# The first norm's shift and scale: from column sums on VectorE to TensorE products in column groups, block by block

## The chip, the cores and the metric

One core of a Trainium2 chip runs the whole program. The metric is the time of one execution on the device in microseconds (us), as the median of the runs. TensorE is the matmul engine, VectorE (DVE), ScalarE (ACT) and GpSimd (POOL) are the elementwise engines, SyncE (SP) issues most transfers.

## The reference

Two transformer blocks over 256 tokens of width 1024. Only the opening of the first one matters here:

```python
mx = (silu(c) @ ada_w + ada_b).reshape(b, 1, 6, D)      # c: (1, 1024), ada_w: (1024, 6144)
mc = (silu(c_ctx) @ ada_w + ada_b).reshape(6, D)
hx = modulate(rmsnorm(x, norm1_g), mx[:, :, 0], mx[:, :, 1])    # h * (1 + scale) + shift
hc = modulate(rmsnorm(ctx, norm1_g), mc[0], mc[1])
ux = hx @ w_in          # w_in: (1024, 4608)
uc = hc @ w_in
```

So the shift (columns 0 to 1023 of ada_w) and the scale (columns 1024 to 2047) are needed for two vectors, c and c_ctx, before the first product with w_in; the other four sixths of ada_w are needed for c alone and later. After this come a gated scan in both directions, a Fourier mix, a convolutional feed-forward block, and a second block with pooling, linear attention, cross attention over a memory and another feed-forward block.

## The kernel before

Activations lie transposed: 128 features on the partitions, 8 tiles k of them, tokens along the row. In the opening a row holds 512 columns, 256 tokens of x and 256 of ctx. Each weight is a chunk of 128 x 1024 fp32 (512 KB), one 128-wide column of the weight matrix with all 8 k tiles beside each other. A chunk goes through four steps: SyncE loads it into a ring of four (raw), ScalarE makes its high part (whi, `splits`), VectorE or GpSimd its low part (wlo, `los`; the function `low_by` says who), and TensorE makes three fp32r products for every k: high times high, high times the operand's low part (hcl), low times the operand's high part (hch). The order of all work is written out by hand, engine by engine; each engine runs its own list in order, and semaphores join them.

The opening runs as follows.

- SyncE (L2412 to L2429): the vectors, x and ctx in two halves each, the identity, then in turn eight rows of blocks of the transposed ada_w (`ada`, for the shift) and eight k blocks of the scale (`scale`), 512 KB each, then the first four weights. The loads of chunks 4 to 7 wait until xr is done.
- ScalarE (`act`, L1367 on): silu of c and c_ctx in two layouts, the squares of the eight tiles (sqs), the root, the copy of the spread inverse root to rsx, then operand k: the ctx half of the scaled tile, and the high part hch of the whole tile.
- GpSimd (`pool`, L2342 on): the sum of the eight squares, then xr = x times rsx for the eight tiles, then low parts of weights (chunks 0 on).
- VectorE (`dve`, L1791 on): for each of 8 tiles of the shift two passes of a multiply-and-add-up operation (`ada_sum`), one for c and one for c_ctx, over the row of silu(c) in PSUM; then the scale's rows are turned on TensorE and amul is made in one piece; then the x half of the scaled tile k, and its low part hcl. The scaled tile (`ht_bank`) lies in PSUM banks 4 to 7.
- TensorE (`pe`, L803 on): spreads the two silu rows over all partitions, makes the scale as two rows of 2 x 512 over all eight k (L832), with the means of the squares and the spreading of the inverse root between, turns the rows by transposes, and starts the first two columns of w_in together (`lins`, one k behind another, the low-weight products two k late), then columns 2 to 7 one at a time (`lin`). After the eight columns come four token-wise chunks, then the rest of the first block.

What runs first after the opening is the forget gates: a sigmoid of each column on ScalarE, two multiply-adds on VectorE, and one `ada_step` on VectorE for the later modulations.

Of the kernel before, what the change touches and what calls it, by code (L numbers as in the profile page):

```python
# [14 lines left out]
KT = 8  # L15
# [39 lines left out]
ADA_OF = [[j] + ([j + 6] if j < 2 else []) for j in range(6)] + [list(range(16 + j, 48, 3)) for j in range(3)]  # L55
# [91 lines left out]
def low_by():  # L147

    out = []
    for j, (name, n, _, _) in enumerate(CHUNKS):  # L150
# [6 lines left out]
        elif (name, n) == ("w_in2", 16):  # L157
            out.append("pool")
        elif j <= ch("w_in", IN_Q + 3):
# [76 lines left out]
def program(nc, D):  # L236
    with ExitStack() as ctx:
# [14 lines left out]
        put("cs", 11, [128, 8, 2])  # L252
        put("sqs", 94 + 16, [128, 8, 512])
        put("crow", 94, [1, 2, 1024])
# [22 lines left out]
        put("ada_buf", Z + 48, [128, 6, 1024])  # L277
        put("ada_sc", Z + 76, [128, 8, 1024])
        put("junk", Z + 32, [128, 1024])
        put("arow", Z + 108, [2, 1024])  # L280
# [83 lines left out]
        class S:  # L364
# [4 lines left out]
            crow = landed("crow", ("c", "ctx"))  # L369
# [3 lines left out]
            ada_in = [landed(f"ada{s}", ADA_OF[s]) for s in range(9)]  # L373
# [7 lines left out]
            rows = signal("rows", ("cb", "cbx", "rows", "turned"))  # L381
# [13 lines left out]
            rowc = signal("rowc", ("crow", "cs", "cb", "arow0"))  # L395
# [40 lines left out]
            ada = signal("ada", list(range(8)) + list(range(16, 48)))  # L436
            both = signal("both")
            inv = signal("inv", NORMS)
            mod = signal("mod", ("amul", "amul2"))
            arow1 = signal("arow1")  # L440
# [46 lines left out]
            ssx = signal("ssx", range(1, 8))  # L487
            xr = signal("xr", range(KT))
# [92 lines left out]
        def ada_at(j):  # L581

            s = next(s for s in range(9) if j in ADA_OF[s])
            if s < 6:
                return s, M["ada_buf"][:, s, :]
            return s, M["ada_kT"][:, s - 6, :] if s < 8 else M["ada_vM"][:, :]

        def ht_bank(k):
            return aux_bank(("ht", k))

        def row_of(who):

            first = 4 if who else 2
            return psum[:, first:first + 2, :].rearrange("p a b -> p (a b)")
# [3 lines left out]
        ht_bank_free = {}  # L598
# [42 lines left out]
        def pe(e):  # L641
# [162 lines left out]
            rows = []  # L804
            for h in range(2):
                slot, _ = lin_ring.take(("rows", h), *((S.arow1, 0) if h else (S.rowc, "arow0")))
                rows.append(banks[slot])
# [16 lines left out]
            for k in range(KT):  # L824
                if k == 3:
                    means("x", M["sqs"][:, 0, :], 4, S.ssx, 7, (S.by_row, "x"))
# [1753 lines left out]
```

## Time and profile before

| | |
|---|---|
| median of 3 runs | 855.45 us (855.01 to 858.16) |
| the profiled execution | 857.55 us, span 855.7 us |
| TensorE busy, weight load | 837.4 us (98%), 762.5 us (89%) |
| VectorE, ScalarE, GpSimd busy | 589.1, 474.4, 436.8 us |
| moved by DMA | 161.36 MB, mean 189 GB/s |

The profile is of one execution. TensorE is written PE, and its weight load PEld. A line number is that of the kernel printed above; where a helper makes the instruction it is the helper's line (L1732 is any tensor_tensor on VectorE, L519 the low part of a weight). An fp32 product shows as two instructions, an fp32r product as one. Times of instructions that wait inside the engine for a port include that wait.

### The profile page before, as it was taken

To read this page: it belongs to the slowest core of one execution; us is meant where nothing else is said; L and a number is where in the kernel's file an instruction comes from. 1 tells how busy PE (TensorE), PEld (TensorE's weight loads), DVE (VectorE), ACT (ScalarE), POOL (GpSimd) and SP (SyncE) were. 2 spreads that over 40 slices of the span, in tenths; PEclk is the share of its full clock that TensorE was granted. 3 is DMA by queue.
4 is the path that set the end of the run, shared out by engine and by line. 5 is a ranking of instruction groups with operands and counts; after the bars stand their busy time and mean duration, and the time that the engine had idled before them with its cause. 6 is when DMAs were issued, how large, how long until landed. Compare 5 with 4: busy or idle time off the path is not lost.

```text
span 855.7 us, 14585 instructions
## 1 busy us (share of the span) xinstructions
PE 837.4 (98%) x5738; PEld 762.5 (89%) x5738; DVE 589.1 (69%) x1186; ACT 474.4 (55%) x787; POOL 436.8 (51%) x210
## 2 busy tenths in 40 slices
PE   7999999999899999999999999999999999999997
PEld 2388899999699999999999988999999888888886
DVE  4897979976667797676767869776547544454445
ACT  4542344442656665555555765555446766666665
POOL 4775512223663478888788400200000688888883
PEclk9999999999999999999999999999999999999999
DMA  9967566655377456556555445364535555565651
GB/s 342 377 229 244 170 245 197 217 187 162 138 227 229 153 173 197 192 175 189 182 179 191 163 148 186 89 210 133 176 119 172 173 173 183 187 197 185 196 187 72
DMA packets 45895, 161.36 MB, mean 189 GB/s; under 512 B 5234, under 2 KB 5506, under 8 KB 45700
## 3 DMA queue, kind: packets, MB, share of 16 engines
q1 hardware_dynamic: 45824, 160.43, 57.1%
q8 instruction: 45, 0.74, 0.3%
q14 instruction: 22, 0.18, 0.1%
q10 hardware_dynamic: 4, 0.01, 0.0%
HBM read 159.37 MB, written 1.05 MB: 187 GB/s over the span
## 4 chain that ended last, share of the span: by engine, by line
PE 87%; DVE 5%; DMA 3%; ACT 3%; issue 1%; POOL 0%; SPq 0%; DVEq 0%; ACTq 0%
PE bank L657 14%; PE bank L662 14%; PE bank L660 13%; PE bank L1036 9%; PE bank L1042 5%; PE bank L1125 2%; PE bank L1127 2%; PE bank L1129 2%; PE bank L1077 2%; PE bank L1075 2%; PE bank L1073 2%; DVE wlo L519 2%; PE bank L935 2%; DMA ada_sc<-in_ada 2%; PE bank L765 1%; PE bank L759 1%
## 5 line engine op out<-in xcount | busy, mean ns | idle before, releaser
L519 POOL TENSOR_TENSOR wlo<-raw,whi 128x1024 fp32r<-128x1024 f32 (+1 forms) x171 | 399.3, 2353 | 374.3 <-ACT whi L1307 374.2
L1307 ACT ACTIVATE whi<-raw 128x1024 fp32r<-128x1024 f32 (+1 forms) x253 | 258.2, 1026 | 62.5 <-PE bank L662 23.6
L1735 DVE SCALAR_TENSOR_TENSOR accs<-bank,vec,accs 128x189 f32<-128x189 f32 (+4 forms) x440 | 161.2, 434 | 71.2 <-ACT accs L1598 71.2
L657 PE MATMUL bank<-h,whi 128*128 128x256 f32 x504 | 143.7, 286 | 0.0
L662 PE MATMUL bank<-h,whi 128*128 128x256 f32 x504 | 142.3, 283 | 0.0
L660 PE MATMUL bank<-h,wlo 128*128 128x256 f32 x496 | 140.5, 283 | 0.7 <-DVE wlo L519 0.7
L519 DVE TENSOR_TENSOR wlo<-raw,whi 128x1024 fp32r<-128x1024 f32 x82 | 99.6, 1227 | 17.5 <-ACT whi L1307 16.9
L657 PEld LDWEIGHTS bank<-h,whi 128*128 128x128 f32 x504 | 96.7, 192 | 0.7 <-issue 0.3
L662 PEld LDWEIGHTS bank<-h,whi 128*128 128x128 f32 x504 | 96.7, 192 | 0.0
L660 PEld LDWEIGHTS bank<-h,wlo 128*128 128x128 f32 x496 | 95.2, 192 | 1.1 <-DVE wlo L519 1.0
L1036 PE MATMUL bank<-h,whi 128*128 128x512 f32 x352 | 88.4, 392 | 0.5 <-DVE gl L1732 0.4
L1036 PEld LDWEIGHTS bank<-h,whi 128*128 128x128 f32 x352 | 64.3, 188 | 13.2 <-DVE gl L1732 0.6
L657 PE MATMUL bank<-hch,whi 128*128 128x256 f32 (+1 forms) x240 | 73.6, 307 | 0.0
L660 PE MATMUL bank<-hch,wlo 128*128 128x256 f32 (+1 forms) x240 | 73.0, 304 | 0.0
L662 PE MATMUL bank<-hcl,whi 128*128 128x256 f32 (+1 forms) x240 | 73.0, 304 | 0.0
L1598 ACT ACTIVATE accs<-bank,vec 128x256 f32<-128x256 f32 x88 | 44.9, 561 | 38.4 <-PE bank L662 32.1
L1732 DVE TENSOR_TENSOR bank<-bank,sq 128x256 f32<-128x256 f32 x44 | 19.0, 432 | 63.7 <-ACT sq L1572 63.7
L1042 PEld LDWEIGHTS bank<-h,wlo 128*128 128x128 f32 x352 | 48.0, 190 | 3.4
L1042 PE MATMUL bank<-h,wlo 128*128 128x256 f32 x352 | 49.1, 282 | 0.0
L660 PEld LDWEIGHTS bank<-hch,wlo 128*128 128x128 f32 x240 | 45.8, 191 | 2.0
L657 PEld LDWEIGHTS bank<-hch,whi 128*128 128x128 f32 x240 | 45.8, 191 | 2.0
L662 PEld LDWEIGHTS bank<-hcl,whi 128*128 128x128 f32 x240 | 45.8, 191 | 1.8
(357 smaller groups left out, 1854.4 us busy)
## 6 DMA issues: line engine op xcount, KB each, us to landing
raw<-in_up SPq DMA_DIRECT2D x88, 512.0 KB, 3.5
raw<-in_w_in SPq DMA_DIRECT2D x45, 512.0 KB, 4.5
raw<-in_down SPq DMA_DIRECT2D x44, 512.0 KB, 3.5
ada_kT<-in_adaT SPq DMA_DIRECT2D x22, 512.0 KB, 4.1
raw<-in_w_out SPq DMA_DIRECT2D x16, 512.0 KB, 4.6
raw<-in_w_in_t SPq DMA_DIRECT2D x12, 512.0 KB, 4.6
ada_vM<-in_adaT SPq DMA_DIRECT2D x10, 512.0 KB, 4.7
ada_buf<-in_adaT SPq DMA_DIRECT2D x8, 512.0 KB, 12.2
```

Of the source, the lines that this page charges most:

```text
L519: return e.tensor_tensor(wlo[:, j % HL, 0:k], raw[:, j % RAW, 0:k], whi[:, j % HL, 0:k].bitcast(F32), ALU.subtract)
L657: e.matmul(ps, wh[:, k, :], xh(k), start=k == 0, stop=False)
L660: e.matmul(ps, wl[:, k, :], xh(k), start=False, stop=False)
L662: t = e.matmul(ps, wh[:, k, :], xl(k), start=False, stop=k == KTILES[name] - 1 and not late)
L935: t = e.matmul(banks[4 + slot][:, h * 128:h * 128 + 128], M["near"][:, h, tile], by_blocks(Q2, h, tile, 1 << v), start=True, stop=True)
L1036: e.matmul(ps, wh[:, k, :], M["h2"][:, k, :, :].rearrange("p v t -> p (v t)"), start=k == 0, stop=False, skip_group_check=True)
L1042: t = e.matmul(ps[:, 0:L], wl[:, k, :], M["h2"][:, k, 0, :], start=False, stop=k == KT - 1, skip_group_check=True)
L1073: e.matmul(ps, wh[:, j, :], gh, start=k == 0 and j % 2 == 0, stop=False, skip_group_check=True)
L1307: e.activation(whi[:, j % HL, 0:(k1 - k0) * 128], raw[:, j % RAW, 0:(k1 - k0) * 128], ACT.Copy).then_inc(S.hi.up(j))
L1598: e.activation(acc_at(t), z_at(f, t), ACT.Identity, scale=conv_weight(f, n, centred(f)), bias=conv_bias(f, n)).then_inc(S.acc0.up((f, t)))
L1732: return e.tensor_tensor(out, a, b, op)
L1735: return e.scalar_tensor_tensor(out=out, in0=a, scalar=s, in1=b, op0=o1, op1=o2)
```

## The change

The shift and the scale come from TensorE, tile by tile of the output, and the first four columns of w_in advance together with them.

- Layout: ada_w's first 2048 columns are stored as eight blocks, one for each output tile k: all 1024 rows against the 128 columns of the shift and the 128 of the scale (8 x 128 x 256, 1 MB).
- TensorE, `mod_rows(k)`: eight fp32 products, one for each 128 rows of ada_w, with a stationary operand of 128 x 32 (silu of c and of c_ctx, and 30 zero columns). Product kb goes to column group 32 * (kb % 4), so the block's result is four partial sums, each on its own 32 partitions of PSUM. ScalarE copies the 128 x 256 to arow (`row`). `turn_rows(k)`: two products of arow with the constant sel, which turns the rows into columns and adds the four partial sums.
- VectorE, `modulation(k)`: bias and norm gain on the two columns of tile k. The sixteen passes of `ada_sum` for the shift are gone.
- ht, the scaled tile, lies in SBUF (`M["ht"]`, two buffers) in place of PSUM.
- VectorE sums the squares in place of GpSimd, makes tile 0 of xr, and makes the low parts of the first four weights (`TOGETHER`) in place of GpSimd. GpSimd makes tiles 1 to 7 of xr.
- ScalarE makes the splits of weights 0 to 3 between its other steps. The tables of Exp and Sqrt are loaded ahead of the squares.
- SyncE loads weight 0, block 0, weights 1 to 3, blocks 1 to 7, weights 4 and 5.
- TensorE runs columns 0 to 3 of w_in together: step k is their twelve products for tile k. Between the halves of step k (k = 1 to 5) stand the turning of block k + 1 and the products of block k + 2. Steps 6 and 7 are run column by column.

```diff
 (TensorE)
+            def mod_rows(k):
+
+                w.wait_ge(S.sc[k], 0)
+                if k:
+                    w.wait_ge(S.arow, k - 1)
+                for kb in range(KT):
+                    g = 32 * (kb % 4)
+                    t = e.matmul(mod_row(k)[g:g + 32, :], M["cs"][:, kb, :], M["ada_sc"][:, k, kb, :], start=kb < 4,
+                                 stop=kb >= 4, tile_position=(0, g))
+                t.then_inc(S.mod_rows.up(k))
+
+            def turn_rows(k):
...
+                for v in range(2):
+                    t = e.matmul(turned_at(k)[:, 2 * v:2 * v + 2], M["arow"][:, k % 2, v * 128:v * 128 + 128],
+                                 col("sel", 0, 2), start=True, stop=True)
...
+            def step(k, which):
+
+                first, last = k == 0, k == KT - 1
+                for c, ps, free in (columns[j] for j in which):
+                    if first:
+                        w.wait_ge(*free)
+                        w.wait_ge(S.hi, c)
+                    w.wait_ge(high, high_event(k))
+                    e.matmul(ps, weights(c)[0][:, k, :], xh(k), start=first, stop=False)
+                for c, ps, _ in (columns[j] for j in which):
+                    w.wait_ge(*lo(c))
+                    e.matmul(ps, weights(c)[1][:, k, :], xh(k), start=False, stop=False)
+                for c, ps, _ in (columns[j] for j in which):
+                    w.wait_ge(low, low_event(k))
+                    t = e.matmul(ps, weights(c)[0][:, k, :], xl(k), start=False, stop=last)
...
+            means("x", M["sqs"][:, 0, :], 4, S.ssx, 7, (S.by_row, "x"))
+            keep_busy(1)
             w.wait_ge(S.rowc, "cs")
...
+            mod_rows(0)
+            spread("x", aux_bank("x"))
+            turn_rows(0)
             keep_busy(2)
...
+            step(0, (0, 1))
+            mod_rows(1)
+            step(0, (2,))
+            turn_rows(1)
+            step(0, (3,))
+            mod_rows(2)
+            for k in range(1, KT - 2):
+                step(k, (0, 1))
+                turn_rows(k + 1)
+                mod_rows(k + 2)
+                step(k, (2, 3))
+            turn_rows(KT - 1)
+            for j in range(TOGETHER):
+                for k in (KT - 2, KT - 1):
+                    step(k, (j,))
...
 (ScalarE)
+            row(0)
+            by_row("x", M["rsx"][:, :], aux_bank("x"))
+            splits(2)
+            operand(0)
+            splits(3)
+            row(1)
             splits(4)
+            operand(1)
+            row(2)
+            for k in range(2, KT):
+                operand(k)
+                if k + 1 < KT:
+                    row(k + 1)
...
 (VectorE)
+            los(1)
+            modulation(0)
+            w.wait_ge(S.by_row, "x")
+            tt(M["xr"][:, 0, :].rearrange("p (v t) -> p v t", v=2), M["xc"][:, :, 0, :],
+               M["rsx"][:, :].rearrange("p (v t) -> p v t", v=2), ALU.mult).then_inc(S.xr0.up(0))
+            scaled(0)
+            los(2)
+            operand_low(0)
+            los(3)
+            los(4)
+            for k in range(1, KT):
+                modulation(k)
+                scaled(k)
+                operand_low(k)
...
 (SyncE)
+            loads(1)
+            modulation(0)
+            loads(4)
+            for k in range(1, KT):
+                modulation(k)
+            loads(RAW + 2)
```

## Rows read from the trace of the kernel before

**Rows 1.** The page: busy time and instructions by engine; the chain by engine.
```profile
PE 837.4 (98%) x5738; PEld 762.5 (89%) x5738; DVE 589.1 (69%) x1186; ACT 474.4 (55%) x787; POOL 436.8 (51%) x210
...
PE 87%; DVE 5%; DMA 3%; ACT 3%; issue 1%; POOL 0%; SPq 0%; DVEq 0%; ACTq 0%
```

**Rows 2.** The chain that ended last, first 70 us: start, length, what.
```profile
12.97 1.28 DVE ada_buf L1757
...
17.18 13.40 DMA ada_sc<-in_ada
...
30.63 1.88 PE bank L832 x4
...
36.60 0.70 PE bank L682 x2
```

**Rows 3.** Timeline of TensorE: start, length, engine, line; columns 2 and 4 start.
```profile
48.29 0.39 PE L657 MATMUL bank<-hch,whi 128*128 128x512 f32 x1
...
59.17 0.39 PE L657 MATMUL bank<-hch,whi 128*128 128x512 f32 x1
```

**Rows 4.** Table of stretches: length, busy PE PEld DVE ACT POOL, clock, DMA share, GB/s.
```profile
25.00:30.00 5.00, 4.27 (x10) 0.51 (x8) 4.93 (x9) 1.00 (x2) 5.00 (x5) 1.00 1.03 410
```

**Rows 5.** Timeline of TensorE's products (first line) and weight loads in the opening.
```profile
4.87 7.16 PE L813 MATMUL bank<-crow,cst 1*128 1x512 f32 x8 [4.87 <-ACT crow L1371]
...
14.46 0.13 PEld L832 LDWEIGHTS bank<-ada_sc,cs 128*2 128x2 f32 x1 [0.72 <-issue]
...
18.61 0.09 PEld L832 LDWEIGHTS bank<-ada_sc,cs 128*2 128x2 f32 x1 [0.34 <-issue]
...
20.41 0.97 PEld L777 LDWEIGHTS bank<-ones,sqs 128*128 128x128 f32 x8 [0.86 <-issue]
...
33.49 0.57 PEld L842 LDWEIGHTS bank<-ident,arow 2*128 2x128 f32 x8 [0.76 <-ACT arow L1391]
```

**Rows 6.** Timeline of ScalarE in the opening.
```profile
7.42 2.19 ACT L1378 ACTIVATE sqs<-xc 128x512 f32<-128x512 f32 x4 [2.49 <-DMA xc<-in_ctxT]
...
33.04 1.99 ACT L1307 ACTIVATE whi<-raw 128x1024 fp32r<-128x1024 f32 x2
...
35.25 0.57 ACT L1395 ACTIVATE bank<-xr,mod,amul 128x256 f32<-128x256 f32 x1 [0.23 <-DVE bank L1814]
...
35.86 0.60 ACT L1398 ACTIVATE hch<-bank 128x512 fp32r<-128x512 f32 x1
```

**Rows 7.** VectorE: timeline, and the page's group of low parts (busy, mean ns).
```profile
37.57 0.69 DVE L1732 TENSOR_TENSOR hcl<-bank,hch 128x512 fp32r<-128x512 f32 x1
...
134.75 1.27 DVE L1732 TENSOR_TENSOR Q<-Q,f 128x512 f32<-128x512 f32 x2
...
L519 DVE TENSOR_TENSOR wlo<-raw,whi 128x1024 fp32r<-128x1024 f32 x82 | 99.6, 1227 | 17.5 <-ACT whi L1307 16.9
```

**Rows 8.** Timeline of GpSimd in the opening.
```profile
8.64 9.75 POOL L2347 TENSOR_TENSOR sqs<-sqs 128x512 f32<-128x512 f32 x7 [8.20 <-ACT sqs L1378]
...
24.57 9.87 POOL L2350 TENSOR_TENSOR xr<-xc,rsx 128x512 f32<-128x512 f32 x8 [6.18 <-ACT rsx L1317]
```

**Rows 9.** Timelines of VectorE and GpSimd, 49 to 58 us and 93 to 98 us.
```profile
49.54 0.43 DVE L1840 TENSOR_SCALAR kk<-f 128x512 f32<-128x512 f32 x1
...
49.88 3.49 DVE L1757 CUSTOM_DVE_ANT_0 ada_kT<-ada_kT,cb,vec 128x1024 f32<-128x1024 f32 x1
...
49.89 8.28 POOL L519 TENSOR_TENSOR wlo<-raw,whi 128x1024 fp32r<-128x1024 f32 x3 [1.46 <-ACT whi L1307]
...
53.31 2.62 DVE L1836 TENSOR_SCALAR f<-sq,lbs 128x512 f32<-128x512 f32 x1
...
93.07 4.56 DVE L1732 TENSOR_TENSOR kk<-kk,suf 128x1024 f32<-128x1024 f32 x2
...
93.21 3.33 POOL L519 TENSOR_TENSOR wlo<-raw,whi 128x1024 fp32r<-128x1024 f32 x1 [3.04 <-ACT whi L1307]
```

**Rows 10.** Timeline of TensorE: the turning of the keys.
```profile
114.21 1.91 PE L882 MATMUL bank<-ident,kk 128*128 128x128 f32 x16
```

More of the change, by code:

```diff
@@ L54 @@
 FPAIRS = [(f, i) for f in range(2) for i in range(NFF)]
-ADA_OF = [[j] + ([j + 6] if j < 2 else []) for j in range(6)] + [list(range(16 + j, 48, 3)) for j in range(3)]
+ADA_OF = [list(range(16 + j, 48, 3)) for j in range(3)]
+TOGETHER = 4
 NVEC1 = VOFF["ffn_conv_b"]
@@ L803, in pe @@
             one_row = cst[0:1, 1:2].broadcast_to((1, 128))
[L804 to L807, printed above, removed]
-            for who, ring, first in ((0, lin_ring, 0), (1, aux_ring, 4)):
-                w.wait_ge(S.const, "cst")
-                w.wait_ge(S.rowc, "crow")
-                for half in range(2):
-                    slot, _ = ring.take(("row", who, half), S.ada, 7)
-                    t = e.matmul(banks[first + slot], one_row, M["crow"][:, who, half * 512:half * 512 + 512], start=True,
-                                 stop=True)
-                t.then_inc(S.rows.up(("cb", "cbx")[who]))
@@ L817, in pe @@
-            w.wait_ge(S.rowc, "cs")
+            w.wait_ge(S.const, "cst")
+            w.wait_ge(S.rowc, "crow")
+            for half in range(2):
+                t = e.matmul(banks[2 + half], one_row, M["crow"][:, half * 512:half * 512 + 512], start=True, stop=True)
+                lin_ring.until[2 + half] = (S.rowc, "cb")
+            t.then_inc(S.rows.up("cb"))
             def keep_busy(n):
                 for _ in range(n):
-                    e.matmul(banks[3], ident[:, :], M["rsx"][:, :], start=True, stop=True)
@@ L845, in pe @@
-            keep_busy(2)
-            for k in range(KT):
-                ht_bank_free[k] = aux_ring.take(("ht", k), S.hcl, k)[1]
-            columns = []
-            for j in range(2):
-                slot, free = lin_ring.take(("ff", j), S.sgf, j)
-                columns.append(("w_in", IN_FF + j, banks[slot][:, :], free))
-            lins(columns, hc_all, 2)
-            for j in range(2, 8):
+                    e.matmul(banks[7], ident[:, :], M["sqs"][:, 7, :], start=True, stop=True)
@@ new lines, in pe @@
+            columns = []
+            for j in range(TOGETHER):
+                slot, free = lin_ring.take(("ff", j), S.sgf, j)
+                columns.append((ch("w_in", IN_FF + j), banks[slot][:, :], free))
+            xh, xl, high, high_event, low, low_event = hc_all
+            def step(k, which):
[12 more added lines that the diff above has]
+                    t = e.matmul(ps, weights(c)[0][:, k, :], xl(k), start=False, stop=last)
+                    if last:
+                        t.then_inc(S.chunk.up(c))
@@ L1808, in dve @@
[L1808 to L1819 removed]
+            ssx = M["sqs"][:, 0, :]
@@ new lines, in scaled, with operand_low @@
+            def scaled(k):
+                w.wait_ge(S.modk, k)
+                w.wait_ge(*((S.xr, k) if k else (S.xr0, 0)))
+                if k > 1:
+                    w.wait_ge(S.hcl, k - 2)
+                e.tensor_scalar(ht_bank(k)[:, 0:L], M["xr"][:, k, 0:L], amul[:, k, 0:1], mod[:, k, 0:1], ALU.mult,
+                                ALU.add).then_inc(S.scaled.up(k))
+            def operand_low(k):
+                w.wait_ge(S.hch, k)
+                tt(M["hcl"][:, k, :], ht_bank(k), M["hch"][:, k, :].bitcast(F32), ALU.subtract).then_inc(S.hcl.up(k))
```

209 lines of the change are left out of this document (93 added, 116 removed), and 2 rows, old and new, of the table VEC.

## The prediction

> **What bounds the kernel now.** I read the page first: TensorE is busy for 98% of the span and is 87% of the chain that ended last, of all the chain's shares the next is VectorE with 5% [rows 1]. So time can be had only where TensorE does no product that the result needs, which is the opening. The chain of the first 70 us [rows 2] runs through transfers, the eight column sums of the shift on VectorE, the last block of the scale at 30.63 us, and operand 0; the first product of w_in starts at 36.60 us. Then TensorE runs without a gap: column 2 starts at 48.29 us and column 4 at 59.17 us, so a column of 24 products takes 5.44 us, 0.227 us each [rows 3]. **The mark.** After the fourth column both kernels do the same work on a full TensorE. I compare the moment when column 4 starts: 59.2 us before. What the change moves that moment by, it moves the end by.
>
> **What is removed.** Sixteen passes of the custom operation on VectorE (1.28 us each) [rows 2], and the wait for them; the whole scale ahead of the first product. The DMA volume stays: eight blocks of 1 MB in place of sixteen of 0.5 MB, plus nothing else but a smaller c row. The queues moved some 410 GB/s here [rows 4]; the last old block landed at 30.6 us [rows 2] after some 10.6 MB. In the new order the first block (3.8 MB) is in at 14 us, the four weights by 18, and the last block (12.7 MB) at 36 us, 2.6 us apart. That is faster than TensorE will use them (below), so the transfers are hidden.
>
> **TensorE's price of a block.** The 16 fp32 products of the scale appear as 32 instructions; a pass over 512 columns took 0.85 us at first and 0.43 us by 18.6 us [rows 5]. The granted clock reads 1.00 in the opening [rows 4], but this halving is that of 2.4 against 1.2 GHz, and came only after TensorE had been at work, on thin operands, since 4.87 us; I read the level by these spacings. A block now has 8 fp32 products of 256 columns, 16 passes of 0.213 us: 3.41 us one after the other, 0.85 us if four column groups always run side by side. Nothing in this trace shows column groups. It does show how closely load and product pairs follow each other when they do nearly nothing: 8 in 0.97 us (0.12 each) for the means, 8 in 0.57 us (0.07 each) for the turning [rows 5]. Sixteen pairs make 1.95 or 1.15 us. I take 2.0 us, from the means, which like the new products are two loads per fp32 product over 128 rows. For the range: 0.85 to 3.41 us. The turning of a block's rows is two fp32 products, four pairs, 0.5 us.
>
> The Trainium skill, in TensorE: Matmul & The Clock Gate, Part 3 (packing small matmuls), has products in different column groups overlapping, 2.38 times for three groups of 32, with starts and ends kept in program order. By that order the second pass of a product, in the same group as its first, would hold back the next group, and a block would be nine passes, an estimate of 1.9 us; no run here shows it yet. The same notes, in TensorEngine Tiling, Key Properties, say that changing the tiling mode drains the engine; the new code changes it twice a block, which would add to the sum what no row prices.
>
> **The opening, step by step.** ScalarE squares the first four tiles from 7.42 us and the rest by 12.2 (0.54 us each, with the copy of the c row, 1.00 us, now behind them; the second four could not start before about 10, when their transfers were in) [rows 6]. VectorE adds them at 0.64 us in place of GpSimd's 1.39 [rows 7, 8]: done at 13.2 where it was 20.4. Means 1.05 us to 14.4; one filler product, at the low clock two passes of 0.85, to 16.1; block 0, at the low clock, 3.8 us (1.7 to 6.8), to 19.9; the four transposes about 0.9 us, to 20.8; the copy to rsx 0.60 us, as for hch [rows 6], and a hand-over, to 21.5. Call this t0. It was 24.5 before, as GpSimd's xr shows [rows 8].
>
> **A wait that was not there.** Before, VectorE's part had an operand or a result in PSUM throughout, and ran undisturbed: its passes stayed at 1.28 us while GpSimd added squares [rows 2, 8]. The change moves ht to SBUF, and gives VectorE tile 0 of xr and the low halves of four weights, all SBUF to SBUF, while GpSimd does tiles 1 to 7 of xr. Rows of a later stage show what that costs [rows 9]: from 49.88 us, with three low halves queued on GpSimd, a custom operation of 1.28 us takes 3.49, and a multiply of about 0.5 us takes 2.62, and GpSimd's three take 8.28 us. At 93.07 us two VectorE products of 1.2 us each take 4.56, with a GpSimd one between them. The two engines take turns, one instruction each, even where VectorE's next one is ready. GpSimd's xr is 1.23 us a tile [rows 8]. VectorE: products of 128x512 0.64, low half 1.22, 128x256 scaling about 0.3 (0.43 for 512 elements), low part of the operand 0.64 to 0.69 [rows 7, 9]. From t0 (P is GpSimd's turn of 1.23; the modulation, 0.5 us first, reads PSUM):
> P, xr 0 to +1.9; P, scaled 0 to +3.4, whereupon ScalarE's 0.60 us make hch 0 at +4.0; P, low of weight 1 to +5.9; P, hcl 0 to +7.8; P, low of weight 2 to +10.2.
> TensorE: columns 0 and 1 of step 0 end at +8.3; block 1 to +10.3; ScalarE copies its rows (about 0.4 us) and only then splits weight 3 (1.00 us), to +11.9. GpSimd has its last turn to +12.7, the low of weight 3 ends at +13.9, and TensorE's column 3 of step 0 at +14.6; block 2 to +16.6. Operand 1 is ready at +15.9. Step 1 starts at t0 + 16.6 = 38.1 us, later than the old kernel's first product.
>
> **The rest to column 4.** From here TensorE has no gap, but has more to do. A step of four columns is 12 products, 2.72 us; with a block 2.0 and a turning 0.52 it is 5.25 us; five of these (steps 1 to 5, blocks 3 to 7) are 26.2. ScalarE has 0.57 + 0.60 + 0.4 us a step [rows 6] and VectorE some 1.6, both hidden under TensorE; if TensorE's share were small the transfers (2.6 us a block) would be next. Then one turning, 0.5 us, steps 6 and 7, 5.44 us, and some 1.5 us in which step 7 waits for its operand: after the turning of block 7 come modulation 0.4, scaling 0.57, hch 0.60 and hcl 0.7, about 2.6 us with hand-overs, against 1.1 us of products to do. Sum: 38.1 + 26.2 + 7.4 = 71.8 us, against 59.2: **12.6 us later**. Column 4's own low half (GpSimd, 2.4 us behind a split of 1.05) ends about when it is wanted, since column 0 ends 4.1 us ahead of column 3. VectorE's work behind the columns has slack: its products with the suffixes ended at 97.6 us [rows 9], and TensorE turns their result at 114.2 [rows 10].
>
> The profiled execution took 857.55 us, its span 855.7; the sum on it gives 870.1. It lay 2.1 us above the median of the runs, 855.45 (855.01 to 858.16), so as a median I forecast 868.0.
>
> **Rivals.**
> A. Column groups overlap better and the pair rate is that of the turning: 1.15 us a block. t0 = 19.5, step 1 at +14.9, five steps of 4.4, plus 7.4: 63.8 us, 4.6 later, 860. For it: the 0.07 us pairs. Against: those load two rows, not 128.
> B. Column groups don't overlap for fp32: 3.41 us a block, 6.8 for block 0. t0 = 24.5, step 1 at +18.8, five of 6.65, plus 7.4: 84.0 us, 24.8 later, 880. For it: every fp32 product here is two passes in a row.
> C. The turn-taking does not strike (GpSimd and VectorE interleave without loss): VectorE's work after t0 shrinks to about 6 us, step 1 at t0 + 12, 33.5 + 26.2 + 7.4 = 67.2, 8 later, 863.5. Rows 9 speak against it.
> D. The other side, faster: four groups always side by side, 0.85 us a block, which with the high clock from the means on gives t0 = 17.6, and VectorE free of GpSimd starts step 1 at 26.3. Then 26.3 + 5 x 4.07 + 7.4 = 54.2 us, 5.0 us earlier, 850.5. It decides where a block costs under 1 us and step 1 starts before 27 us, since TensorE needs 28 us after that even then. A block this short with step 1 near 31 would make no change. Against it stand rows 9; I keep its chance above C's because a price of a block far from any row could carry it alone, with a shorter tail than I work out. By the skill's rule of concurrent groups taken whole, without my reading of the order of passes, the block is this 0.85 us.
>
> **How the numbers follow.** Forecast 0.42, A 0.20, B 0.10, C 0.11, D 0.17. The forecast's own range is 862 to 874 (a block at 1.5 to 2.3 us is worth 4 us either way, clock and turns 2). Leaving out B and the earlier half of D gives 850 to 876. About 0.5%, 4.3 us, is what a measurement of this kernel can tell from none: faster 0.17, all of D; A lies on the border and gives most of same, 0.13; slower 0.70.
>
> **What would show it.** In the profile after: t0 (the copy to rsx) near 21.5; VectorE's subtractions and xr 0 at 1.2 us above their own time while GpSimd is at xr; the sixteen instructions of a block taking 2.0 us between two steps; step 1 near 38; column 4 near 72. A block under 1.2 us, or VectorE's operations at their plain length beside GpSimd, makes it wrong.

## Result and profile after

| | before | after |
|---|---|---|
| median of 4 runs | 856.81 us (855.01 to 859.82) | 870.92 us (867.78 to 872.04) |
| the profiled execution, its span | 857.55, 855.7 us | 870.18, 868.3 us |
| start of step 1 / start of column 4 | - / 59.17 us | 37.77 / 67.03 us |

The ratio is 1.0155 with a 95% interval of 1.0112 to 1.0198: 14.1 us slower in medians, 12.6 us in the two profiled spans. The forecast was 12.6 us. The total came out, but by luck: two of its terms didn't, and they cancelled.

From the page of the changed kernel, busy time by engine and the chain that ended last:

```profile
PE 838.0 (97%) x5854; PEld 769.7 (89%) x5854; DVE 586.8 (68%) x1180; ACT 477.1 (55%) x794; POOL 421.1 (48%) x199
...
PE 80%; DVE 12%; ACT 3%; DMA 3%; issue 1%; POOL 0%; SPq 0%; DVEq 0%; ACTq 0%; POOLq 0%
```

Against [rows 1] TensorE's busy time is the same within 0.6 us, and the chain's share of VectorE went from 5% to 12%, some 60 us more: TensorE now depends on VectorE for longer stretches. The changed kernel in its opening, timelines of VectorE and of GpSimd (start, length, engine, line, out<-in, count):

```profile
22.74 1.17 DVE L1869 TENSOR_SCALAR ht<-xr,amul,mod 128x256 f32<-128x256 f32 x1
23.83 2.29 DVE L527 TENSOR_TENSOR wlo<-raw,whi 128x1024 fp32r<-128x1024 f32 x1
26.04 1.76 DVE L1791 TENSOR_TENSOR hcl<-ht,hch 128x512 fp32r<-128x512 f32 x1
27.72 2.29 DVE L527 TENSOR_TENSOR wlo<-raw,whi 128x1024 fp32r<-128x1024 f32 x1
32.37 2.33 DVE L527 TENSOR_TENSOR wlo<-raw,whi 128x1024 fp32r<-128x1024 f32 x1 [2.35 <-ACT whi L1348]
...
21.96 11.65 POOL L2415 TENSOR_TENSOR xr<-xc,rsx 128x512 f32<-128x512 f32 x7 [20.92 <-ACT rsx L1358]
```

The turn-taking is there. A low half of 1.22 us takes 2.29, the low part of the operand 1.76 in place of 0.69, and GpSimd's seven tiles take 1.66 us each, not the 1.23 of [rows 8]. Only xr 0, which I had expected to wait for GpSimd's first tile, kept its plain 0.68 us (21.95, started 0.01 us ahead of GpSimd's).

TensorE in the same kernel, and the granted clock in the table of stretches (length, busy PE PEld DVE ACT POOL, clock, DMA share, GB/s):

```profile
29.00 1.94 PE L831 MATMUL bank<-ada_sc,cs 128*32 128x256 f32 x16
...
34.76 0.80 PE L862 MATMUL bank<-hch,wlo 128*128 128x512 f32 x1 [1.87 <-DVE wlo L527]
...
37.77 0.81 PE L859 MATMUL bank<-hch,whi 128*128 128x512 f32 x2
...
44.06 1.07 PE L831 MATMUL bank<-ada_sc,cs 128*32 128x256 f32 x16
45.06 0.74 PE L859 MATMUL bank<-hch,whi 128*128 128x512 f32 x2
...
67.03 0.39 PE L665 MATMUL bank<-hch,whi 128*128 128x512 f32 x1
```
```profile
25.00:30.00 5.00, 3.36 (x18) 1.46 (x21) 5.00 (x3) 0.58 (x1) 5.00 (x4) 0.77 1.02 424
30.00:35.00 5.00, 3.03 (x21) 1.70 (x14) 2.65 (x4) 1.33 (x2) 3.62 (x3) 0.84 1.00 412
35.00:40.00 5.00, 5.00 (x32) 2.75 (x36) 1.24 (x4) 1.62 (x3) 0.00 (x0) 0.70 1.03 409
```

Two things stand here that the forecast did not have. Where before the clock stayed at 1.00 from 20 to 40 us (25 to 30 us in [rows 4]), it falls to the low level while TensorE waits in step 0 (0.77, 0.84, 0.70 in stretches of 5 us). And a block of the scale and shift takes 1.00 us from its start to the next product at the high level, half of the 2.0 that I had put in; at the low level it takes 1.9. Column 4 starts 7.9 us later than in [rows 3], not 12.6.

The missing 4.7 us are lost later, at about 124 us. VectorE, then TensorE, of the changed kernel:

```profile
63.81 0.55 DVE L1906 TENSOR_SCALAR f<-sq,lbs 128x512 f32<-128x512 f32 x1 [0.60 <-ACT sq L1468]
...
120.51 1.28 DVE L1821 CUSTOM_DVE_ANT_0 ada_kT<-ada_kT,cb,vec 128x1024 f32<-128x1024 f32 x1 [1.24 <-DMA ada_kT<-in_adaT]
...
126.69 1.28 DVE L1821 CUSTOM_DVE_ANT_0 ada_kT<-ada_kT,cb,vec 128x1024 f32<-128x1024 f32 x1 [1.20 <-DMA ada_kT<-in_adaT]
...
127.90 0.42 DVE L1791 TENSOR_TENSOR qx<-bank,sq 128x256 f32<-128x256 f32 x1
```
```profile
122.14 1.91 PE L923 MATMUL bank<-ident,kk 128*128 128x128 f32 x16
128.47 0.77 PE L767 MATMUL bank<-whi,hch 128*128 128x512 f32 x1 [4.42 <-DVE qx L1791]
129.03 0.63 PE L769 MATMUL bank<-whi,hcl 128*128 128x512 f32 x1
...
136.42 3.73 PE L935 MATMUL bank<-V,kcT 128*128 128x128 f32 x32
```

and the lines of the kernel before that answer to them:

```profile
48.96 0.55 DVE L1836 TENSOR_SCALAR f<-sq,lbs 128x512 f32<-128x512 f32 x1 [0.30 <-ACT sq L1409]
...
81.77 0.55 DVE L1836 TENSOR_SCALAR f<-sq,lbs 128x512 f32<-128x512 f32 x1 [3.23 <-ACT sq L1409]
...
113.52 0.42 DVE L1732 TENSOR_TENSOR qx<-bank,sq 128x256 f32<-128x256 f32 x1
...
121.42 3.73 PE L894 MATMUL bank<-V,kcT 128*128 128x128 f32 x32
```

VectorE's first forget gate started 10.2 us ahead of column 4 before (48.96 against 59.17), since columns 0 and 1 were finished early; now the four columns end one close behind another, and it starts 3.2 us ahead (63.81 against 67.03). So VectorE is 14.4 us later when it gives the first qx (113.52 to 127.90), while TensorE is only 7.9 us later when it has turned the keys (114.21 in [rows 10], 122.14 here). Between the two stands VectorE's list: gates, suffixes, and eight ada_steps ahead of qx, three of which wait for a transfer in both kernels (3.6 us in all after, two of the rows above, and 2.8 before); from the first gate to qx 0 it takes as long as it did (64.6 us before, 64.1 after) and starts 14.9 us later (48.96 to 63.81).

That the length is the same is a sum of changes. Before, VectorE had caught up with the columns and waited 4.2 us in all for the sigmoids of the last two gates (3.23 of it at 81.77 above); after, it is behind and never waits for one. Against that, ten of its 24 instructions in the gates are lengthened by GpSimd's turns where seven were, 6.3 us more, while behind the gates GpSimd's turns cost it 3.2 us less (the products with the suffixes take 2.36 us, not the 4.56 of [rows 9]). GpSimd's low halves now start with the gates and come four in a row, where [rows 9] had three. GpSimd of the changed kernel:

```profile
64.74 10.84 POOL L527 TENSOR_TENSOR wlo<-raw,whi 128x1024 fp32r<-128x1024 f32 x4 [31.12 <-ACT whi L1348]
```

So the turn-taking has a part in this second loss too: with no more of it in VectorE's list than before, 3.1 us less in all, TensorE's wait of 4.4 us would be one of about 1.3. That is an estimate from the rows; no run took this part away alone.

TensorE waits 4.42 us, and after the wait runs twelve products at 0.43 us in place of 0.23, 2.4 us more, before it is at the high level again (granted clock 0.67 and 0.64 from 125 to 135 us). At the next common mark the changed kernel is 15.0 us behind (121.42 to 136.42). Of this 2.4 us come back near 228 us, where TensorE waited for ScalarE before and hardly does after. The kernel before, then after, TensorE:

```profile
224.30 0.70 PE L977 MATMUL bank<-PP,dft 128*128 128x256 f32 x2 [0.52 <-ACT PP L1484]
...
226.65 0.70 PE L977 MATMUL bank<-PP,dft 128*128 128x256 f32 x2 [1.22 <-ACT PP L1484]
...
228.20 0.39 PE L657 MATMUL bank<-fmh,whi 128*128 128x256 f32 x1 [0.41 <-DVE fml L1732]
```
```profile
240.78 0.39 PE L665 MATMUL bank<-fmh,whi 128*128 128x256 f32 x1 [0.28 <-DVE fml L1791]
```

The books of the profiled executions close: 7.9 at column 4, 7.1 at 124 us, 2.4 back by 240.78 (12.6 after 228.20), 12.6 in the span.

### The profile page after: what moved, and what is told of

The parts are those of the page before. It is cut to its first block, busy times and chain, and to the rows that moved or that the text cites. A ratio compares the mean times of both kernels' runs of the same rounds, so it can differ in the third digit from the quotient of the medians.

```text
span 868.3 us, 14829 instructions
## 1 busy us (share of the span) xinstructions
PE 838.0 (97%) x5854; PEld 769.7 (89%) x5854; DVE 586.8 (68%) x1180; ACT 477.1 (55%) x794; POOL 421.1 (48%) x199
## 3 DMA queue, kind: packets, MB, share of 16 engines
HBM read 159.37 MB, written 1.05 MB: 185 GB/s over the span
## 4 chain that ended last, share of the span: by engine, by line
PE 80%; DVE 12%; ACT 3%; DMA 3%; issue 1%; POOL 0%; SPq 0%; DVEq 0%; ACTq 0%; POOLq 0%
PE bank L665 12%; PE bank L670 12%; PE bank L668 11%; PE bank L1077 9%; PE bank L1083 5%; PE bank L1166 2%; PE bank L1168 2%; PE bank L1170 2%; PE bank L1118 2%; PE bank L1116 2%; PE bank L1114 2%; DVE wlo L527 2%; DVE ada_kT L1821 2%; PE bank L976 2%; DVE f L1906 1%
## 5 line engine op out<-in xcount | busy, mean ns | idle before, releaser
L527 POOL TENSOR_TENSOR wlo<-raw,whi 128x1024 fp32r<-128x1024 f32 (+1 forms) x167 | 389.5, 2351 | 398.4 <-ACT whi L1348 398.3
L527 DVE TENSOR_TENSOR wlo<-raw,whi 128x1024 fp32r<-128x1024 f32 x86 | 107.8, 1265 | 20.5 <-ACT whi L1348 19.9
L665 PE MATMUL bank<-hch,whi 128*128 128x256 f32 (+1 forms) x224 | 67.4, 301 | 0.0
L668 PE MATMUL bank<-hch,wlo 128*128 128x256 f32 (+1 forms) x224 | 66.8, 298 | 0.0
L670 PE MATMUL bank<-hcl,whi 128*128 128x256 f32 (+1 forms) x224 | 66.8, 298 | 0.0
L1624 ACT ACTIVATE gh<-bank 128x256 fp32r<-128x256 f32 x44 | 17.0, 386 | 52.9 <-DVE bank L1791 52.9
L1114 PE MATMUL bank<-gh,whi 128*128 128x256 f32 x160 | 45.3, 283 | 0.0
L1116 PE MATMUL bank<-gh,wlo 128*128 128x256 f32 x160 | 45.3, 283 | 0.0
```

Source lines behind the costliest of these rows:

```text
L527: return e.tensor_tensor(wlo[:, j % HL, 0:k], raw[:, j % RAW, 0:k], whi[:, j % HL, 0:k].bitcast(F32), ALU.subtract)
L665: e.matmul(ps, wh[:, k, :], xh(k), start=k == 0, stop=False)
L668: e.matmul(ps, wl[:, k, :], xh(k), start=False, stop=False)
L670: t = e.matmul(ps, wh[:, k, :], xl(k), start=False, stop=k == KTILES[name] - 1 and not late)
L1114: e.matmul(ps, wh[:, j, :], gh, start=k == 0 and j % 2 == 0, stop=False, skip_group_check=True)
L1116: e.matmul(ps, wl[:, j, :], gh, start=False, stop=False, skip_group_check=True)
```

## Experiments

Each experiment starts from the changed kernel. The median of the kernel before was 856.29 us beside the first four and 855.82 beside the last three. "Column 4" is the start of its first product on TensorE.

### GpSimd taken out of the opening

Tiles 1 to 7 of xr go to VectorE, one step ahead of their use; GpSimd has nothing to do there until the low half of weight 4.

```diff
 (VectorE)
+            def normed(k):
+                w.wait_ge(S.by_row, "x")
+                tt(M["xr"][:, k, :]..., M["xc"][:, :, k, :], M["rsx"][:, :]..., ALU.mult).then_inc(S.xr.up(k))
...
             los(3)
+            normed(1)
             los(4)
             for k in range(1, KT):
                 modulation(k)
                 scaled(k)
                 operand_low(k)
+                if k + 1 < KT:
+                    normed(k + 1)
 (GpSimd)
-            w.wait_ge(S.by_row, "x")
-            for k in range(1, KT):
-                e.tensor_tensor(M["xr"][:, k, :]...)
```

> The changed kernel with tiles 1 to 7 of xr made by VectorE, each one step ahead (tile 1 before the low half of weight 3), in place of GpSimd, which then has nothing to do until weight 4. Theory: step 1 starts at 37.8 us because VectorE and GpSimd take turns, one instruction each, so VectorE's seven instructions of the opening take 1.1 to 1.2 us more than their own time. Then here they take their own time (low half 1.2 in place of 2.3 us, scaled tile 0.4 in place of 1.17, hcl 0.69 in place of 1.76), hcl 0 ends near 25 in place of 27.8, and step 1 starts at 33 (32 to 34), column 4 about 4.5 us earlier than 67.0, at 62.5; the whole kernel 864 to 867 us, ratio to the kernel before near 1.010, since VectorE's late backlog only moves with it. Rival: TensorE's own chain (block 1, its copy, the split of weight 3, the low clock) sets step 1, and it stays at 36 us or later with the time within 1.5 us of 870.

Measured: 862.66 us, ratio 1.008 (1.0058 to 1.0103), 8.3 us less than the changed kernel and a little below the range that I had named. VectorE and TensorE of this kernel:

```profile
22.59 0.41 DVE L1869 TENSOR_SCALAR ht<-xr,amul,mod 128x256 f32<-128x256 f32 x1
22.92 1.22 DVE L527 TENSOR_TENSOR wlo<-raw,whi 128x1024 fp32r<-128x1024 f32 x1
24.06 0.68 DVE L1791 TENSOR_TENSOR hcl<-ht,hch 128x512 fp32r<-128x512 f32 x1
```
```profile
30.98 0.73 PE L859 MATMUL bank<-hch,whi 128*128 128x512 f32 x2
...
60.19 0.39 PE L665 MATMUL bank<-hch,whi 128*128 128x512 f32 x1
```

The same instructions take 0.41, 1.22 and 0.68 us where they took 1.17, 2.29 and 1.76. VectorE has seven more tiles to do and step 1 still starts 6.8 us earlier, and column 4 with it. It is more than the 4.5 us that I expected, for which I hadn't counted the clock: it stayed at 1.00 from 20 to 40 us. The late wait is unchanged, 4.40 us. So the turn-taking is worth 6.8 us of the 7.9 by which column 4 was late, the fall of the clock that it brings about included; the next but last experiment parts the two.

### The late wait taken away alone

Five of the ada_steps get their weights early, into buffers of their own, and run in steps 2 to 6, where VectorE idles; three are left ahead of qx. The opening's turn-taking stays.

```diff
 (VectorE, the loop over k in the opening)
                 operand_low(k)
+                if 2 <= k < 7:
+                    ada_step()
...
-            for _ in range(8):
+            for _ in range(8 - (EARLY - 16)):      # EARLY = 21, so 3
                 ada_step()
 (SyncE: their transfers right behind the sixth weight, ahead of the wait for xr)
             for j in (16, 17, 18):
                 ada(j)
             loads(HL + RAW)
+            for j in (19, 20):
+                w.wait_ge(S.ada, j - 3)
+                ada(j)
```

> The changed kernel with five of the sixteen ada_steps that follow the columns (tiles 16 to 20 of the later modulations, 1.28 us each) done by VectorE in steps 2 to 6 of the opening, where it is idle, from three buffers of their own; the eight behind the suffix products become three. Theory: of the 12.6 us that the profiled execution lost, 7.9 are lost by column 4, and the rest because the product qx 0 comes at 127.9 us, behind eight ada_steps, so TensorE waits 4.4 us at 124 us and then runs 12 products at 0.43 us in place of 0.23. Then here the wait of TensorE before the Fourier chunks is gone or under 0.5 us, the low clock after it too, column 4 stays at 67 us, and the kernel takes 863 to 866 us, ratio near 1.009. Rival: the late loss comes from the chunks' loads and DMA landing times, which shift with it: the wait stays above 3 us, and the time within 1.5 us of 870.

Measured: 863.44 us, ratio 1.0083 (1.0061 to 1.0104). Column 4 starts at 67.00 us, as in the changed kernel, and TensorE of this kernel at the place of the wait:

```profile
122.16 1.91 PE L928 MATMUL bank<-ident,kk 128*128 128x128 f32 x16
123.83 0.47 PE L772 MATMUL bank<-whi,hch 128*128 128x512 f32 x1
124.14 0.39 PE L774 MATMUL bank<-whi,hcl 128*128 128x512 f32 x1
```

The keys are turned at the same moment (122.16 against 122.14), the wait is gone and so is the low clock behind it, and the whole is 7.5 us shorter. The second loss is its own, and what stands ahead of qx in VectorE's list makes it. This edit took five ada_steps and the waits for their transfers away from there at once; the fifth experiment changes the order alone.

### All products of a block in one column group

```diff
                 for kb in range(KT):
-                    g = 32 * (kb % 4)
-                    t = e.matmul(mod_row(k)[g:g + 32, :], ..., start=kb < 4, stop=kb >= 4, tile_position=(0, g))
+                    t = e.matmul(mod_row(k)[0:32, :], ..., start=kb == 0, stop=kb == 7, tile_position=(0, 0))
```

The copies and turnings take the 32 rows that are left.

> The changed kernel with all eight products of a block in column group 0 (summed in PSUM on 32 partitions, the turning over 32 rows), so that none can run beside another. Theory: in the changed kernel the groups overlap fully; a block is 16 passes of 0.213 us one after the other here, 3.4 us at the high clock and 6.8 at the low one, in place of 1.0 and 1.9. Then steps 1 to 5 take 6.7 us in place of 4.33, column 4 starts 12 us later from these alone and 4 to 10 us more from blocks 0 to 2 (83 to 89 us), and the kernel takes 885 to 892 us. Rival: most of a block is the fixed cost of 16 load and product pairs (0.06 us each) and the groups hardly matter: a block stays under 1.5 us and the time under 875.

Measured: 892.10 us (2 runs), ratio 1.042 (1.0389 to 1.045), at the upper end of what I expected. TensorE of this kernel:

```profile
54.30 3.64 PE L830 MATMUL bank<-ada_sc,cs 128*32 128x256 f32 x16
57.88 0.73 PE L858 MATMUL bank<-hch,whi 128*128 128x512 f32 x2
...
88.19 0.39 PE L665 MATMUL bank<-hch,whi 128*128 128x512 f32 x1
```

From a block's start to the next product it is 3.58 us in one group and 1.00 us in four, 3.6 times. Sixteen passes in 1.00 us is 0.063 each, under a third of what one pass takes alone (3.58 / 16 = 0.224). So the second pass of an fp32 product does not hold back the other groups: had each group's two passes to go by in program order, as the prediction reasoned, the block could not be shorter than nine passes, 2.0 us. With five blocks in the steps the block's price is 4.4 of the 4.8 us by which the forecast was too late at column 4 (71.8 against 67.03).

### The step order mended, with five early ada_steps

The first experiment, and with it: the filler product ahead of block 0 taken out, block 1 ahead of step 0, block 2 ahead of its column 2, the weights split ahead of the rows they had waited behind, VectorE's low halves each one place earlier, the last two steps in an order that lets operand 7 come. The five early ada_steps of the second experiment stand in steps 2 to 6.

```diff
 (TensorE)
-            keep_busy(1)
             w.wait_ge(S.rowc, "cs")
...
-            keep_busy(2)
-            step(0, (0, 1))
             mod_rows(1)
-            step(0, (2,))
+            keep_busy(1)
+            step(0, (0, 1))
             turn_rows(1)
-            step(0, (3,))
             mod_rows(2)
+            step(0, (2,))
+            step(0, (3,))
...
-            for j in range(TOGETHER):
-                for k in (KT - 2, KT - 1):
-                    step(k, (j,))
+            step(KT - 2, (0, 1))
+            step(KT - 2, (2,))
+            step(KT - 1, (0,))
+            step(KT - 2, (3,))
+            for j in range(1, TOGETHER):
+                step(KT - 1, (j,))
 (ScalarE)
+            splits(2)
             row(0)
             by_row("x", M["rsx"][:, :], aux_bank("x"))
-            splits(2)
-            operand(0)
             splits(3)
+            operand(0)
             row(1)
```

> Everything together: xr on VectorE, five ada_steps early, and the opening's order changed: block 0 straight behind the means (no filler product), block 1 and one filler in place of two fillers, the low half of weight 1 ahead of the modulation, splits 1 and 2 ahead of the copies, the blocks' products of step 0 ahead of its columns 2 and 3, and steps 6 and 7 interleaved so that the wait for operand 7 is covered. Theory: rsx is ready at 20 us, step 1 starts at 27 to 29 us, then five steps of 4.33 and 6.9 us put column 4 at 55.5 to 58 us, 1 to 3.5 us ahead of the kernel before; without the late wait the kernel takes 852 to 856 us, ratio 0.996 to 1.000. Rival: TensorE's added work for blocks and turnings (8 of 1.5 us) can't be won back by an earlier start, because the low clock returns in the gaps of step 0: step 1 after 30 us, column 4 after 59, ratio above 1.002.

Measured: 866.16 us (862.85 to 867.99; the profiled execution is the fastest of the four), ratio 1.0112 (1.0083 to 1.0142), a miss. Step 1 started at 27.04 us as expected. VectorE, then TensorE, of this kernel:

```profile
40.61 1.29 DVE L1828 CUSTOM_DVE_ANT_0 ada_early<-ada_early,cb,vec 128x1024 f32<-128x1024 f32 x1 [8.61 <-DMA ada_early<-in_adaT]
...
43.57 1.22 PE L864 MATMUL bank<-hch,whi 128*128 128x512 f32 x2 [7.72 <-ACT hch L1453]
```

The queues moved some 410 GB/s throughout; the early ada weights, issued at 19.71 us, stood behind the blocks and had landed only by 40.6, and VectorE, now 11 us ahead of where it had been, waited 8.61 us for them with all later operands queued behind. TensorE lost 7.7 us, and the clock fell behind the wait (0.52 from 40 to 45 us). In the second experiment the first of the same ada_steps ran at 41.60 us without a wait, since step 2 came later there. The steps belong only where their data has landed.

### The ada_steps parted around qx

```diff
-            for _ in range(8):
+            for _ in range(5):
                 ada_step()
             for h in range(4):
                 los(ch("w_in", IN_Q + h) + HL)
                 w.wait_ge(S.sg, ("q", h))
                 tt(qx[:, h, :], ...).then_inc(S.qx.up(h))
+                if h < 3:
+                    ada_step()
```

> The changed kernel with VectorE's order behind the suffix products changed and nothing else: five ada_steps, then qx 0 to 2 each followed by one ada_step, then qx 3, in place of eight ada_steps and then the four qx. Theory: the eight ada_steps ahead of qx 0 make TensorE's late wait of 4.4 us and the low clock behind it. Then qx 0 is done near 122 us, ahead of the 124 at which TensorE has need of its bank, the wait is under 0.5 us, and the kernel takes 864 to 866 us as with the five early ada_steps (863.4, ratio 1.008). Rival: VectorE's later work (ksum, the products with Q) is what TensorE waits for next, since the total before it is the same; a wait of 2 to 4 us appears there and the time stays at 867 to 870 us.

Measured: 865.92 us, ratio 1.0117 (1.0098 to 1.0135). TensorE, then VectorE, of this kernel:

```profile
125.39 0.74 PE L773 MATMUL bank<-wlo,hch 128*128 128x512 f32 x2 [0.65 <-DVE wlo L527]
...
130.24 0.73 PE L773 MATMUL bank<-wlo,hch 128*128 128x512 f32 x2 [1.81 <-DVE wlo L527]
```
```profile
126.79 3.40 DVE L527 TENSOR_TENSOR wlo<-raw,whi 128x1024 fp32r<-128x1024 f32 x1
```

Two shorter waits, 2.5 us together, take the place of 4.42, and the clock doesn't fall behind them. The gain over the changed kernel is 5.0 us: the time is the one that the theory named, but its wait of under 0.5 us is not. VectorE's first qx comes in time for the first product. The first wait left follows an ada_step that waited 1.05 us for its transfer; the second is for a low half that took 3.40 us in place of 1.22, one turn of GpSimd's, and at its plain length it would have been ready in time. Order alone gives back about two thirds of the late loss.

### TensorE kept at work in step 0, turn-taking left

Products without a use (into a free bank) fill TensorE's waits in step 0; VectorE and GpSimd are as in the changed kernel.

```diff
+            w.wait_ge(S.by_row, "x")
-            keep_busy(2)
-            step(0, (0, 1))
+            keep_busy(3)
+            step(0, (0, 1), 1)
             mod_rows(1)
             step(0, (2,))
             turn_rows(1)
-            step(0, (3,))
+            step(0, (3,), 2)
 (the last argument of step: so many products without a use between its high and its low weights; in the call with columns 0 and 1 one more ahead of hcl)
```

> The changed kernel with filler products (an fp32 product of 512 columns, 0.86 us at the high clock) in TensorE's waits of step 0: one more ahead of it, one before each of the waits for a low weight and for hcl 0, two before the low of weight 3. The turn-taking of VectorE and GpSimd stays. Theory: in the changed kernel TensorE's clock is low from 26 to 38 us, because TensorE waits 5 us in pieces there; blocks 1 and 2 take 1.94 us in place of 1.07 and the products 0.43 in place of 0.23, of which some 2 us are on the path to step 1. Then here blocks 1 and 2 take 1.07 us and step 1 starts at 36 us or a little before, the time 867 to 869 us. Rival: the low halves that end at 34.7 us set step 1, and the clock changes it by the last block and the last three products only: under 1.3 us, 869.5 us.

Measured: 866.61 us, ratio 1.0132 (1.0115 to 1.015), a little under the range that I had named. The table of stretches, then TensorE, of this kernel:

```profile
25.00:30.00 5.00, 4.81 (x27) 2.28 (x27) 5.00 (x3) 0.93 (x2) 5.00 (x4) 1.00 1.01 421
30.00:35.00 5.00, 4.94 (x31) 2.66 (x31) 3.21 (x6) 2.42 (x5) 3.58 (x2) 1.00 1.00 412
```
```profile
28.72 1.07 PE L831 MATMUL bank<-ada_sc,cs 128*32 128x256 f32 x16
...
34.86 0.73 PE L859 MATMUL bank<-hch,whi 128*128 128x512 f32 x2
...
64.07 0.39 PE L665 MATMUL bank<-hch,whi 128*128 128x512 f32 x1
```

The granted clock reads 1.00 where it read 0.77 and 0.84, block 1 takes 1.07 us in place of 1.94, step 1 starts at 34.86 us, and column 4 starts 3.0 us earlier. In this profile the means had started 0.5 us earlier for another reason (14.25 against 14.78), so the clock is worth some 2.4 us; of the 6.8 us of the first experiment about 4.4 are left for the turn-taking itself, if the two add up.

### Both losses removed

The first experiment and the fourth's order; three early ada_steps, in steps 5 to 7, when their weights have landed; two ahead of qx and three between the qx; weight 4 split ahead of the first sigmoid, with its low half on VectorE.

```diff
-EARLY = 21
+EARLY = 19
...
                 if k + 1 < KT:
                     normed(k + 1)
-                if 2 <= k < 7:
+                if k >= 5:
                     ada_step()
...
-            for _ in range(8 - (EARLY - 16)):
+            for _ in range(2):
                 ada_step()
             for h in range(4):
...
+                if h < 3:
+                    ada_step()
 (ScalarE, behind the last operand; VectorE, ahead of the first gate)
+            splits(TOGETHER + 1)
+            los(TOGETHER + 1)
```

(the lines taken away are those of the fourth experiment)

> The reordered kernel with its flaw mended: there the first early ada_step stood in step 2 on VectorE, its data landed only at 40.6 us behind the blocks, and TensorE waited 7.7 us for the operand queued behind it. Here three ada_steps (not five) stand in steps 5 to 7, when their data has landed, and the other five are two before and three between the four qx; weight 4 is split before the first sigmoid and its low half is VectorE's. Theory: step 1 starts at 27 us as in the reordered kernel, and with five steps of 4.33 us, 0.5, 5.4 and about 0.9 us of waits column 4 starts at 55 to 56 us, 3 to 4 us before the old kernel's 59.2; the late wait is under 0.5 us, and the kernel takes 852 to 854 us, ratio 0.994 to 0.998. Rival: VectorE's shorter lead over TensorE (its gate work starts 3 us ahead of column 4 in place of 10) is lost again later whatever the order, a wait of 2 to 4 us appears at the first scan products, and the ratio is 0.999 to 1.003.

Measured: 853.94 us (8 runs, 851.49 to 855.38) against 855.82 (13 runs), ratio 0.997 (0.9956 to 0.9984). TensorE of this kernel:

```profile
19.89 1.07 PE L836 MATMUL bank<-ada_sc,cs 128*32 128x256 f32 x16 [0.98 <-DMA ada_sc<-in_ada]
...
26.17 0.63 PE L864 MATMUL bank<-hch,whi 128*128 128x512 f32 x2
...
55.66 0.50 PE L670 MATMUL bank<-hch,whi 128*128 128x512 f32 x1 [0.37 <-ACT sq L1476]
...
118.06 3.73 PE L942 MATMUL bank<-V,kcT 128*128 128x128 f32 x32
```

Column 4 starts 3.5 us earlier than before the change (59.17), and the mark of 121.42 is reached 3.4 us earlier: here what column 4 gains is kept. It is 17 us faster than the changed kernel and 0.3% faster than the kernel before. The interval leaves 1 out, though the gain is smaller than the 0.5% that I had named as the bound. Between the means and column 4 TensorE's longest wait is now for the transfer of block 1 (0.98 us at 19.89; the fourth experiment had 0.78 there): the queue shows on TensorE, as it never did in the changed kernel's blocks.

## Why the prediction was right, and where it wasn't

The forecast of 868.0 us was 2.9 us under the median measured, 870.92, which its range of 862 to 874 held. Of the signs that it named, the copy to rsx near 21.5, VectorE's subtractions some 1.1 us above their own time, and step 1 near 38 came. Three didn't: xr 0 was not lengthened, a block took 1.0 us and not 2.0, and column 4 came at 67.0 and not near 72. It had also said that a block under 1.2 us would make it wrong, and by that sentence its sum was wrong though its total was right. By its own steps:

- **t0, confirmed.** The copy to rsx ended at 21.9 us (21.5 foretold). Inside, the means came 1.4 us late, since the second four squares waited longer for their transfer, and took 0.8 us longer. Block 0 took 1.9 us, not 3.8. These are two errors of about 2 us that cancelled.
- **The turn-taking, confirmed and shown.** VectorE's instructions were lengthened to the sizes that [rows 9] gave, and plain without GpSimd beside them. Step 1 at 37.77 us (38.1 foretold). In it blocks 1 and 2 took 1.9 us, near the 2.0 that I had put in, but for a reason I had not: the low clock doubled a price half as large. So the agreement at step 1 is partly luck: with the clock held up it was 34.86 us.
- **The price of a block, mis-sized.** 2.0 us foretold, 1.0 measured. This is nearly the whole of the error at column 4: from step 1 to the end of step 5 it was 21.8 us (37.77 to 59.55) where I had 26.2, and the rest to column 4 was 7.5 where I had 7.4. What failed in this step is the choice of the row: the pairs of the means (0.12 us each) were taken as a floor for any pair over 128 rows. The range for it, 0.85 to 3.41, held the value. The Trainium skill, in TensorE: Matmul & The Clock Gate, Part 3 (packing small matmuls), has products in different column groups overlap, 2.38 times for three groups; here sixteen passes in four groups overlap too, 3.6 times. My reading of its program order on top, by which a block would be nine passes, failed.
- **"VectorE's work behind the columns has slack", wrong.** I read the slack from the suffix products at 97.6 us and the turning of the keys at 114.2. The work with the least slack was the next in VectorE's list, qx, which TensorE could use from 115.9 us on (the turning takes 1.7 us) and which was done at 113.94: 1.9 us of slack. The work in front of it starts from a moment (the end of columns 0 and 1) that the change moved by 14.9 us, not by 7.9, and GpSimd's turns take 3.1 us more of it than before; I had followed the turn-taking no further than the opening.
- **"What the change moves that moment by, it moves the end by", wrong with it.** 7.1 us were added behind column 4 and 2.4 given back. That the total came out all the same is luck: the block's price and what went with it put 4.7 us too much at column 4, and 4.7 too few were put behind it.
- **The clock, left out.** I took block 0 at the low level and everything behind it at the high one. Waits in step 0 brought it down, some 2.4 us, and the wait at 124 us did again, 2.4 us (twelve products at 0.43 in place of 0.23).

The rivals. **A** (a block of 1.15 us) had the price of a block nearly right and the time wrong, for the two reasons just named: its column 4, 63.8 us, is what the sixth experiment gave with the clock held up (64.07). **B** (no overlap) did not hold either: a block takes 1.00 us in the changed kernel, and 3.58 where the third experiment made B true, which gave 892 us where B had 880. **C** (no turn-taking) did not hold; made true in the first experiment it gave 862.7 us, near C's 863.5, by the same two errors that cancelled. **D** (faster) named the point rightly: a block under about 1 us and step 1 before 27 us. The change came to the first (1.00 us) and missed the second by 11 us; the last experiment has both, step 1 at 26.17, and is the only one that is faster than the kernel before.

Left open: whether earlier loads of the ada weights alone, with VectorE's list as it is, would have taken the 3.6 us of its waits out of the 4.42; no run tried it, nor one with the scaled tile back in PSUM and nothing else changed. And the 2.4 us given back near 228 us were read from the traces and not isolated: the last experiment's profiled span is 6.0 us shorter than that of before, of which 3.4 are made by its mark at 118.06, while the medians are 1.9 us apart, so what a profile shows gained behind that mark is not safe.

## What to carry to other kernels

Two engines can both have time to spare and still cost each other a doubling: before work is moved, ask which operand kept an instruction off the shared path (here a tile in PSUM) and who is at work beside it. Measure a change at more than one mark: the end alone gave 12.6 us, as foretold; column 4 (7.9) and the mark behind the late wait (15.0) showed that one term was half of what was foretold and that another loss was new. When a group of results is made to end together, look for whoever lived from the first of them ending early, and follow its list to the next thing that TensorE waits for.

## What the runs showed of the hardware

- Column groups side by side: sixteen fp32 passes of 256 columns take 1.00 us in four groups and 3.58 us in one, with both at the high clock. The first pair of products after a block takes 0.74 us against 0.62 elsewhere. That is some 0.1 us a block, and it isn't shown to be the price of the column groups: the first product behind the turning of the keys takes 0.47 us in place of 0.39 too (115.87 in the kernel before), with no column group near.
- VectorE and GpSimd alternate one instruction each when both work from SBUF to SBUF: 0.41, 0.68 and 1.22 us become 1.17, 1.76 and 2.29, and are plain again where GpSimd has nothing to do (first experiment). The Trainium skill, in SBUF — State Buffer, "SBUF: two separate sides", calls the port that the two share an exclusive lock for a whole instruction; the trace agrees, and a stream of GpSimd's gets its turn after each of VectorE's four instructions from 22.74 to 30 us.
- The clock: with waits of 1.36, 0.46, 1.18 and 1.87 us in and ahead of step 0 the granted clock read 0.77, 0.84 and 0.70 in three stretches of 5 us and a block took 1.94 us, not 1.07; after one wait of 4.4 us twelve products ran at the low level of 1.2 GHz. With the waits of step 0 filled it read 1.00 from 25 to 35 us. The two waits of the fifth experiment, 0.65 and 1.81 us at 125 and 130 us, left it at 1.00, so the length of a single gap doesn't decide it.
